# One remainder in four of the down projections: an accumulating DMA in place of a VectorE subtraction

## The reference

```
def swiglu_ffn(x, norm_pre, w_gate, w_up, w_down, norm_post):
    h = rms_norm(x, norm_pre)
    a = jax.nn.silu(h @ w_gate) * (h @ w_up)      # (256, 5632)
    return x + rms_norm(a @ w_down, norm_post)    # w_down: (5632, 2048)
```

## Time and profile before

| | |
|---|---|
| median of 2 runs | 2025.39 us (2025.27 and 2025.52) |
| span of the profiled execution | 2021.2 us |
| PE busy | 1998.1 us, 99% of the span |
| DVE busy | 1189.4 us, 59% |
| ACT busy | 983.6 us, 49% |
| POOL busy | 199.5 us, 10% |
| mean granted TensorE clock | 0.996 of full speed |
| share of the 16 DMA engines in the feed-forward slices | 0.5 to 0.7 |

### The profile page before, as it was taken

How to read it: one execution, slowest core, us unless ns; L and a number is a source line. 1 busy time by engine, 2 the same in 40 slices (tenths; PEclk the granted TensorE clock), 3 DMA queues, 4 the chain that set the end, 5 groups by cost and what they waited for, 6 DMA issues and landing times.

```text
span 2021.2 us, 27616 instructions
## 1 busy us (share of the span) xinstructions
PE 1998.1 (99%) x9842; PEld 1696.4 (84%) x9842; DVE 1189.4 (59%) x1499; ACT 983.6 (49%) x1150; POOL 199.5 (10%) x123
## 2 busy tenths in 40 slices
PE   9999999999999999999999999999999999999998
PEld 7898888888888888888899977888888888888886
DVE  5755565555555554444799975655555555554444
ACT  6544464545455443433744464454444444443433
POOL 1000000000000000000689830000000000000000
PEclk9999999999999999999999989999999999999999
DMA  9745566766666765555355525566666666665554
GB/s 324 238 144 191 176 217 221 222 216 213 217 216 219 219 219 195 192 196 191 127 189 179 177 94 198 168 238 217 211 215 222 216 222 212 217 212 194 193 192 146
DMA packets 137966, 407.58 MB, mean 202 GB/s; under 512 B 15330, under 2 KB 38498, under 8 KB 137378
## 3 DMA queue, kind: packets, MB, share of 16 engines
q1 hardware_dynamic: 135796, 396.84, 59.6%
q0 software_dynamic: 2096, 9.70, 1.4%
HBM read 392.84 MB, written 13.63 MB: 201 GB/s over the span
## 4 chain that ended last, share of the span: by engine, by line
PE 88%; DVE 9%; ACT 1%; DMA 1%; issue 1%; SPq 0%; POOL 0%; DVEq 0%; ACTq 0%
PE acc L1297 83%; DVE acc L1211 7%; PE acc L1308 1%; PE acc L1310 1%; PE acc L1309 1%; PE acc L1538 1%; DMA raw<-in_units 1%; PE acc L1349 0%; ACT w_hi L570 0%; DVE gated L1198 0%; DVE conv L1216 0%; DVE conv L1211 0%; DVE w_lo L915 0%; DVE conv L1249 0%; PE acc L1347 0%
## 5 line engine op out<-in xcount | busy, mean ns | idle before, releaser
L917 DVE SCALAR_TENSOR_TENSOR w_lo<-raw,vecs,w_hi 128x1024 fp32r<-128x1024 f32 x398 | 509.2, 1282 | 437.3 <-ACT w_hi L570 437.1
L570 ACT ACTIVATE w_hi<-raw,vecs 128x1024 fp32r<-128x1024 f32 x398 | 457.8, 1152 | 514.2 <-PE acc L1297 471.9
L570 ACT ACTIVATE w_hi<-raw 128x1024 fp32r<-128x1024 f32 x304 | 321.2, 1059 | 397.2 <-PE acc L1297 352.3
L915 DVE TENSOR_TENSOR w_lo<-raw,w_hi 128x1024 fp32r<-128x1024 f32 x236 | 288.9, 1225 | 320.8 <-ACT w_hi L570 320.8
L1297 PE MATMUL acc<-w_hi,xT_hi 128*128 128x512 f32 x1528 | 472.0, 390 | 2.2 <-DVE w_lo L917 1.7
L1297 PE MATMUL acc<-w_lo,xT_hi 128*128 128x512 f32 x1528 | 470.5, 389 | 0.0
L1297 PE MATMUL acc<-w_hi,xT_lo 128*128 128x512 f32 x1528 | 470.5, 389 | 0.0
L1297 PEld LDWEIGHTS acc<-w_hi,xT_hi 128*128 128x128 f32 x1528 | 285.7, 188 | 63.7 <-issue 3.4
L1297 PEld LDWEIGHTS acc<-w_hi,xT_lo 128*128 128x128 f32 x1528 | 286.8, 188 | 59.8
L1297 PEld LDWEIGHTS acc<-w_lo,xT_hi 128*128 128x128 f32 x1528 | 286.8, 188 | 59.7
L1297 PE MATMUL acc<-w_lo,hT_hi 128*128 128x512 f32 x704 | 217.4, 389 | 0.0
(11 more groups left out here) (171 smaller groups left out, 1444.3 us busy)
## 6 DMA issues: line engine op xcount, KB each, us to landing
raw<-in_units SPq DMA_DIRECT2D x702, 512.0 KB, 3.8
hid_turned_blocks<-tok SPq DMA_DIRECT2D x44, 256.0 KB, 2.8
tok<-hid_turned_blocks SPq DMA_DIRECT2D x176, 64.0 KB, 2.8
gpost<-in_post POOLq DMA_DIRECT2D x4, 1024.0 KB, 6.0
x<-in_x POOLq DMA_DIRECT2D x4, 512.0 KB, 11.1
c_raw<-in_consts POOLq DMA_DIRECT2D x4, 512.0 KB, 7.3
out<-x SPq DMA_DIRECT2D x8, 256.0 KB, 2.8
xT_raw<-in_xT SPq DMA_DIRECT2D x3, 512.0 KB, 8.9
```

The source lines that it names most:

```text
L570: nc.scalar.activation(w_hi[:, s, :], raw[:, s, :], ACT.Copy, scale=scale).then_inc(hi_ready, 1)
L915: ins = nc.vector.tensor_tensor(w_lo[:, s, :], raw[:, s, :], w_hi[:, s, :], ALU.subtract)
L917: ins = nc.vector.scalar_tensor_tensor(w_lo[:, s, :], raw[:, s, :], vecs[:, gain:gain + 1], w_hi[:, s, :], ALU.mult, ALU.subtract)
```

## The change

ACT and DVE use a new `split_down` in the two loops of each down projection, quads 3 to 21. Slots 0 to 2 are as before. In slot 3 ACT, after `w_hi[3]`, reads `raw[3]` again and writes its rounded negative into `w_lo[3]`. POOL waits for that (`neg_hi_ready`) and issues a DMA that loads the same 512 KB unit from DRAM once more and adds it to what `w_lo[3]` holds. DVE waits for the DMA (`raw_added`) and copies one column of a constant, [128, 1], into `added_mark`, which raises `lo_ready` in the order in which PE and SP count it. PE's and SP's code is unchanged. The first three down quads, the gate and up weights and all other stages are unchanged.

```diff
+        added_mark = sb("added_mark", [P, 1])
+        neg_hi_ready = sem("neg_hi_ready")
+        raw_added = sem("raw_added")
...
@@ gpsimd @@
+            def add_raw(layer, q0):
+
+                for n in range(Q_DOWN - 3):
+                    pool.wait_ge(neg_hi_ready, (Q_DOWN - 3) * layer + n + 1)
+                    pool.dma_start(w_lo[:, 3, :], d_units[(q0 + Q_FF + 3 + n) * 4 + 3], accum_op=ALU.add).then_inc(raw_added, 16)
...
             load_post(1)
+            add_raw(0, Q_F0)
             norm_out(1)
...
             load_post(3)
+            add_raw(1, Q_F1)
             norm_out(3)
...
@@ scalar @@
+                def split_down(q):
+
+                    for s in range(4):
+                        split(q, s)
+                    nc.scalar.activation(w_lo[:, 3, :], raw[:, 3, :], ACT.Copy, scale=-1.0).then_inc(neg_hi_ready, 1)
...
                 with act.Fori(qd + 3, qd + Q_DOWN // 2 + 1) as q:
-                    split_quad(q)
+                    split_down(q)
                 square_y(e, par, 0, (0, 1))
                 square_y(e, par, 1, (0, 1))
                 with act.Fori(qd + Q_DOWN // 2 + 1, qd + Q_DOWN) as q:
-                    split_quad(q)
+                    split_down(q)
...
@@ vector @@
+                def split_down(q):
+
+                    for s in range(3):
+                        split(q, s)
+                    dve.wait_ge(raw_added, q * 16 + 16 * ((Q_DOWN - 3) * layer + 1 - (q0 + Q_FF + 3)))
+                    nc.vector.tensor_copy(added_mark[:], pow_exp[:]).then_inc(lo_ready, 1)
...
                 with dve.Fori(qd + 3, qd + Q_DOWN // 2 + 1) as q:
-                    split_quad(q)
+                    split_down(q)
                 gain_y(e, par, 0, (0, 1))
                 gain_y(e, par, 1, (0, 1))
                 with dve.Fori(qd + Q_DOWN // 2 + 1, qd + Q_DOWN) as q:
-                    split_quad(q)
+                    split_down(q)
```

## The result

The changed kernel takes 2118.67 us (2118.43 and 2118.91) against 2025.39: a ratio of 1.046, 95% interval 1.0443 to 1.0477. That is slower by 93.3 us, inside the stated range, but twice the 45.8 that I had forecast.

The account below looks back on a forecast made before the run. PE was taken to bound the kernel until slot 3's loop, 5.90 us plus a 6.0 us DMA, outlasted PE's 10.88 us quad. 22.9 us a layer, 45.8 for both, on 2025.4 gave 2071 us; range 2030 to 2190.

Parts of the forecast that it names:

- PE sets the pace, a lighter DVE is worth nothing: Whole kernel: PE busy 1998.1 of 2021.2 us; removing 38 DVE subtractions, 46.7 us, is worth 0.
- The chain of slot 3 and its first quad: From slot 3's w_hi copy to PE's start: 2.38 us plus the DMA's time, hidden while that DMA is below 5.58 us.
- The loop through the raw load: Down loops, mark to mark: 5.90 us plus the DMA's time; above 4.98 us of DMA it, not PE, sets the pace.
- The last quad: Each layer's last down quad reads slot 3 4.08 us sooner, so its chain is late by the DMA's time less 1.5 us.
- X = 6.0: Accumulating DMA, issue to landing: taken as 6.0 us, giving a delay of 22.9 us a layer, 45.8 for both.
- DMA traffic: costs nothing: Down loops: raw loads fill 58.6% of the DMA engines, 88% with the accumulation, still below full, so no cost.
- the `gpost` row: Earlier trace's 1024 KB DMA on POOL's queue, beside raw loads: 5.5 us at best, 6.0 median, 8.5 worst.
- The small terms: Short pieces of slot 3's round, such as 0.08 us from ACT to POOL's start; each 0.1 us worth 3.8 us.
- rival 3: Down loops: each wait of PE drops its clock to the 1.2 GHz level, 76 us more, 2147 us; chance 0.04.
- Rival 2: Accumulating DMA slow, each row waiting for its own SBUF read: 7.5 to 11.1 us, total 2128 to 2265 us; chance 0.27.
- Rival 1: Accumulating DMA lands within 4.98 us, so only the last quads cost: 2030 to 2032 us; chance 0.17.

Follow-up runs that it names:

- the early load: Changed kernel, but SP loads slot 3's next raw unit once ACT has read the last for the negated copy, not after the addition landed: 2159.12 us, ratio 1.0669.
- thin raw loads: Changed kernel with raw loads of slots 0 to 2 cut to 256 of 1024 columns in down quads with an addition: 2061.72 us, ratio 1.0189.

## Why the prediction was right or wrong

- **PE sets the pace, a lighter DVE is worth nothing.** Right. With the additions hidden the time is that of before.
- **The chain of slot 3 and its first quad.** Right in form. The first addition of each layer took 5.4 and 5.5 us and was in time.
- **The loop through the raw load.** Right as the piece that the diff does not show: the chain rows above are its terms, and my 3.4 us for the raw load was 3.25 in them. 29 of 36 rounds went through the load and 7 through PE. Wrong in saying that nothing of PE's was in it: the round by way of PE is only 0.4 us shorter, and the early load showed that removing the one leaves the other.
- **The last quad.** Right, and confirmed by itself: 13 us for both layers.
- **X = 6.0 and "DMA traffic: costs nothing".** This is the step that failed. I had 5.5 at best from the `gpost` row, and 5.4 is what an addition takes alone. I then took the median, 6.0, as if it were the addition's own weight, and argued from shares (88%, "still below full") and from one load that it had nothing beside it. But the raw loads that had queued behind DVE's wait are still moving when it starts, 0.51 MB beside its 0.52 in the rows above. In the rounds the DMA took 6.87 us: 0.8 of the 1.24 us that a round was longer than forecast. The engine share below full, 84% in those rows, did not tell how long one transfer in it takes.
- **The small terms.** POOL starts a DMA 0.30 us after ACT's end, where I had read 0.08 from a row of a computation, not of a DMA: 0.2 a round. From the mark to ACT's copy it was another 0.2 over the forecast, but that is the clock (rival 3): in the 28 rounds at full clock it was 3.73, as forecast. And the raw load and its issue occur 36 times, not 38, so 0.1 us there is worth 3.6 and not the 3.8 that I gave for any term.
- **Rival 2, the slow addition.** Not so: by itself it takes 5.4 us. X above 7.5 occurred in 6 of the 38 additions only. **Rival 1, hidden**: no, but it is what happens once the chain is moved. The estimate of 4.4 us by the Trainium skill (DMA: Bandwidth & Descriptors, "Anatomy of one DMA") stays below every addition of 512 KB here, 5.1 us at the least; the trace does not agree. The Trainium skill's other rule (Collectives: The Full Stack, "The bandwidth ceiling", that a reduce step runs at half a copy's rate because of its two reads) fits what the trace shows: 3.04 against 1.61 us of the engines, 1.9 times. That the second read is the reason is not shown by itself.
- **Rival 3, the clock.** It happens, and mostly cancels. PE waited 3.37 us until 877.52; the next windows show a granted clock between the levels, 0.70 and 0.74, so part of each at 1.2 GHz, and then 2.4 GHz again (columns as in the earlier trace rows):

```profile
877.00:880.00 3.00, 2.48 (x7) 2.01 (x8) 2.60 (x6) 0.00 (x0) 0.00 (x0) 0.70 0.40 141
880.00:883.00 3.00, 3.00 (x11) 2.36 (x11) 3.00 (x4) 0.84 (x1) 0.00 (x0) 0.74 0.30 105
883.00:886.00 3.00, 3.00 (x15) 2.47 (x14) 0.45 (x1) 2.22 (x3) 0.85 (x1) 1.00 0.89 289
```

The first 3 us of a round show such a clock, 0.50 to 0.77, in 8 of the 36 rounds: the 7 that went through PE, and one more. In the other 28 it was 1.00. In the 8, ACT's copy came 4.4 to 5.0 us after the mark instead of 3.6. But then fewer raw loads were left beside the addition (0.24 to 0.42 MB in 6 of the 8), and it took 5.8 on average instead of 7.2: rounds of 13.0 against 13.2. So these spells did not lengthen the loop. Behind the two last quads the lower clock goes with the 1.4 us a layer named above. PE's busy time grew by 28.5 us; all these spells are a part of that.

## What to carry to other kernels

When work is moved from an idle engine to a DMA, follow the buffer once round: who is told that it is free, what is loaded then, and what waits for that. A chain that closes on itself pays its excess in every round, here 2.45 us a DMA. Begun sooner in a second buffer, the same 38 DMAs cost 0.16% of the time, and with every second quad free of one, a DMA cost 0.8 us. And take a DMA's duration from a row with the same neighbours: those that its own wait will bunch beside it are not in the trace of before.

## What the runs showed of the hardware

- An accumulating DMA of 512 KB into SBUF holds the 16 DMA engines for 3.04 us (2.8 to 3.3 in the other kernels), a copy of the same on the same queue for 1.61, and an addition of half the columns for 1.62; half of one takes as long as a whole copy, 5.0 and 4.9 us to the mark.
- From POOL's issue it lands after 5.4 to 5.5 us at the median with little beside it (thin raw loads, every second quad), and after 7.0 to 8.1 beside whole raw loads. POOL's instruction takes 0.85 us for an addition and 0.53 for a copy.
- In layer 0 one or two additions at the turn from the first loop to the second were among the longest: 8.7 us in the changed kernel, 7.0 and 6.5 with thin raw loads, 6.9 with half additions. In layer 1 it was 8.0, 5.3 and 6.3 there. The cause stays open.
- A raw load of 512 KB took 3.4 us at the median in layer 0's down loops before the change and 5.3 with the additions in two buffers (762 to 965 us), and PE did not wait for it.
- After a mark's wait the granted clock was between 0.50 and 0.77 over 3 us in 8 of 36 rounds, and ACT's copy, which waits for PE, came 1.1 us later in these.
